# Strassen products for the last two chunks of four feed forward stages, and splits of 2048 columns

## The chip, the core and the metric

The kernel runs on one core of a Trainium2 chip. The metric is the device time of one execution in microseconds (us). The kernel before took 1417.25 us, the median of three runs (1417.22 to 1417.32).

## What is computed

Two transformer-like blocks one after the other on x (256 tokens x 1024), all in float32. The feed forward part is what the change is about:

```python
D_MODEL = 1024; SEQ = 256; D_FF = 2816
def swiglu(x, w_in, w_out):
    a, b = jnp.split(x @ w_in, 2, axis=-1)
    return (jax.nn.silu(a) * b) @ w_out
# first block, two layers l = 0, 1, each:
h = h + 0.5 * rms_norm(swiglu(rms_norm(h, g[0]), ffn1_w_in[l], ffn1_w_out[l]), g[1])
h = h + rms_norm(mixer_l(rms_norm(h, g[2])), g[3])
h = h + 0.5 * rms_norm(swiglu(rms_norm(h, g[4]), ffn2_w_in[l], ffn2_w_out[l]), g[5])
# second block: mod = silu(c) @ w_ada + b_ada, an attention/retention mixer, then
ffn = jnp.dot(jax.nn.silu(jnp.dot(h2, w_ffn_gate)) * jnp.dot(h2, w_ffn_up), w_ffn_down)
x = x + gate2 * ffn
```

## The kernel before

**Stages.** There are eight stages, 0 to 7. Stages 0, 2, 3, 5 and 7 are feed forward, 1 and 4 the mixers of the first block, 6 the mixer of the second. The tokens are two halves of 128 (tok 0 and 1), and these are the rows of every matmul's output.

**Units and half units.** All weights are streamed from HBM once, in units of 4 blocks of 128 rows x 512 columns (1 MB). `plan` lists the units in order. A unit goes to one of three ring buffers (`raw`, `load_unit`, L480), which SyncE (SP) loads when the unit three before it has been split. A unit has two half units (`subs`, index j, 1024 columns of SBUF). ScalarE writes `whi`, the float32r value of the half unit (`split_hi`, L508), and VectorE writes `wlo`, the rest (`split_lo`, L524). There are seven slots for half units (NSPL). Both engines run up to five half units (LOOK) ahead of the place in their own program where TensorE's half unit j stands (`ahead`). TensorE makes three matmuls of 512 columns for each block and token half: x high by w high, x high by w low, x low by w high (`products`, L700), so 12 for a half unit.

**A feed forward stage.** The inner 2 x 2816 columns are cut into 11 chunks of 256 + 256 columns (chunk c, two units, 4 half units). After a chunk ScalarE takes silu of one half (L1094) and VectorE multiplies by the other, the gate (L1100), which frees the chunk's PSUM bank. Every two chunks TensorE turns the result (`pe_hid_two`, L1155; the eleventh alone in `pe_hid`), ScalarE and VectorE split it into `gh` and `gl`. Then follows the down part, 22 half units, in groups; the last LAG half units make their tok 0 passes first, and the next stage's first transposes come between.

**Strassen in stage 7.** Two neighbouring chunks, 8 and 9, are one 256 x 1024 by 1024 x 1024 product, cut in 2 x 2 blocks and made from 7 products p1 to p7 instead of 8. `sequence` places one product after each of seven chunks. A product is one unit (12 matmuls in all, `pe_product`, L778). p2 goes through the ring. The others have a buffer of their own: `rows` (x1) for p1, p5, p6 and p4, `work` (x2) for p3 and p7. GpSimd (POOL) issues their loads (`pool_strassen`); for p5, p4 and p7 the DMA adds to what is in the buffer, in two halves. p6's weights are the sum of both buffers, which VectorE makes (`dve_t2`, L543). The sums of x are made in `dve_sx` and `dve_sx_lo` (2048 columns), and results are combined in `act_part` and `dve_combine`. Within such a stage all ordinary chunks use the same two PSUM banks, the products four others.

**The second block's modulation.** w_ada (24 MB) is loaded during stages 0, 2, 3 and 5 in 96 tiles, `adat`, through SP's queue, two buffers: a tile's issue waits until VectorE has added the tile two before it (`ada_add`, L618), which it does right after a split. Eight tiles are followed by a store, a reload and a chain of small sums (`ada_sum`, L621). `ada_units` says at which units; steps are 10 units apart.

Each engine's instructions are in program order, and a wait holds all behind it.

Of the kernel before, what the change touches and what calls it, by code (L numbers as in the profile page):

```python
# [115 lines left out]
def program(nc, T, const_at, out):  # L116
    ctx = ExitStack()
    with ctx:
# [25 lines left out]
        whi = [sb(f"whi{i}", 1024, F32R) for i in range(NSPL)]  # L144
        wlo = [sb(f"wlo{i}", 1024, F32R) for i in range(NSPL)]
# [136 lines left out]
        STRASSEN = (7,)  # L282
        PAIR = 8
# [221 lines left out]

        at = {"hi": 0, "lo": 0}
# [17 lines left out]
        def split_lo(e, upto):  # L524

            while at["lo"] < min(upto, NSUB):
                j = at["lo"]
                u, k, m, n = subs[j]
                if j in sum_before:
                    dve_t2(e, sum_before[j])  # L530
                e.wait_ge(*whi_made.at(j))
                e.tensor_tensor(split_of(wlo, j), raw_of(j), split_of(whi, j).bitcast(F32), ALU.subtract  # L532
                                ).then_inc(*wlo_made.up(j))
# [6 lines left out]

        sum_before = {JP[st, "p6"] - 3: st for st in STRASSEN}

# [311 lines left out]
        def pe_down(e, key, j0, XH, XL, nk, new, readers, at=None, late=None, lag=3, then=None):  # L854
# [18 lines left out]
            for i in range(len(order)):  # L873
# [6 lines left out]
                held.append(i)  # L880
                if i < len(order) - lag and not late or late and len(held) >= lag and i < len(order) - 1:
# [205 lines left out]
        def act_silu(e, st, c, tok):  # L1087
# [4 lines left out]
            if c >= 2 and tok == 0:  # L1092
                e.wait_ge(*hid_turned.at(st, turn_of(c - 2)))
# [19 lines left out]
        def act_silu_pair(e, st, tok):  # L1113
            e.wait_ge(*(product_done(st, "p4" if tok else "p2")))
            if tok == 0:
                e.wait_ge(*hid_turned.at(st, PAIR - 2))
# [11 lines left out]
        def turn_of(c):  # L1128

            return c if c == 10 else c - c % 2  # L1130

        def pe_hid(e, st):
            ps = tb.next(("hid", st, 10), (glo_made, st, 10))
            for done in tb.freed:
                e.wait_ge(*done)
            e.wait_ge(*gated.at(st, 10, 1))
# [4 lines left out]
            last.then_inc(*hid_turned.up(st, 10))  # L1141

        def pe_hid_two(e, st, c):
# [7 lines left out]
            for b in range(8):  # L1151
                n, j, tok = b // 4, b % 4 // 2, b % 2
                for half in range(2):
                    r = slice(half * 64, (half + 1) * 64)
                    last = e.transpose(pst[:, half * 512 + b * 64:half * 512 + (b + 1) * 64],  # L1155
                                       hid[(c + n) % 2][r, tok * 512 + j * P:tok * 512 + (j + 1) * P], ident[r, r])
# [8 lines left out]
        def act_ghi(e, st, c):  # L1165
            e.wait_ge(*hid_turned.at(st, c))
            if c == 10:
                e.activation(gh[:, 5120:5632], tb.of("hid", st, c)[:, :], ACT.Copy).then_inc(*ghi_made.up(st, c))
# [3 lines left out]
        def dve_glo(e, st, c):  # L1172
            e.wait_ge(*ghi_made.at(st, c))
            if c == 10:
                e.tensor_tensor(gl[:, 5120:5632], tb.of("hid", st, c)[:, :], gh[:, 5120:5632].bitcast(F32), ALU.subtract
# [6 lines left out]
        def pe_ffn_in(e, st):  # L1182
# [8 lines left out]
            for c in sequence(st)[2:]:  # L1191
                if c in BLOCK:
                    pe_product(e, st, c, base)
                    if c == "p4":
                        pe_hid_two(e, st, PAIR - 2)
                    continue

                def at(i, c=c):
                    if c % 2 == 0 and i == (3 if st in STRASSEN and c == 10 else 2):
# [11 lines left out]
        def pe_ffn(e, st):  # L1211
# [9 lines left out]
            pe_down(e, ("f", st), j1, gh, gl, 22,  # L1221
                    lambda q, tok: (ghi_made.at(st, turn_of(q // 2)), glo_made.at(st, turn_of(q // 2))), readers, at, lag=LAG[st],
# [1829 lines left out]
```

## Time and profile before

| | |
|---|---|
| median of 3 runs | 1417.25 us |
| the profiled execution | 1416.94 us |
| its span, first to last instruction | 1415.1 us |
| TensorE busy | 1401.8 us, 99% |
| VectorE busy | 956.5 us, 68% |
| ScalarE busy | 731.7 us, 52% |
| GpSimd busy | 160.1 us, 11% |
| moved by DMA | 288.24 MB, 204 GB/s |
| granted TensorE clock | 0.999 |

Busy times are unions of instructions of one engine. A matmul's own duration (390 ns at 512 columns) overlaps the next one's; the distance between starts is what it costs.

### The profile page before, as it was taken

To read this page: it belongs to the slowest core of one execution; us is meant where nothing else is said; L and a number is where in the kernel's file an instruction comes from. 1 tells how busy PE (TensorE), PEld (TensorE's weight loads), DVE (VectorE), ACT (ScalarE), POOL (GpSimd) and SP (SyncE) were. 2 spreads that over 40 slices of the span, in tenths; PEclk is the share of its full clock that TensorE was granted. 3 is DMA by queue.
4 is the path that set the end of the run, shared out by engine and by line. 5 is a ranking of instruction groups with operands and counts; after the bars stand their busy time and mean duration, and the time that the engine had idled before them with its cause. 6 is when DMAs were issued, how large, how long until landed. Compare 5 with 4: busy or idle time off the path is not lost.

```text
span 1415.1 us, 19090 instructions
## 1 busy us (share of the span) xinstructions
PE 1401.8 (99%) x7327; PEld 1147.2 (81%) x7327; DVE 956.5 (68%) x1307; ACT 731.7 (52%) x1050; POOL 160.1 (11%) x242
## 2 busy tenths in 40 slices
PE   9999999999999999999999999999999999999997
PEld 7888888688888888888878888888877788888886
DVE  6666567886676667665787757755568566786654
ACT  6444455564443445543665545445655634655542
POOL 1600010000000000000172100000542110011000
PEclk9999999999999999999999999999999999999999
DMA  9585755256876778868544688764845355588551
GB/s 318 199 253 198 262 203 207 68 171 207 251 242 215 231 228 265 252 210 264 187 150 148 203 210 256 255 211 140 238 160 197 121 178 179 171 242 211 178 209 59
DMA packets 234857, 288.24 MB, mean 204 GB/s; under 512 B 37076, under 2 KB 156672, under 8 KB 234768
## 3 DMA queue, kind: packets, MB, share of 16 engines
q1 hardware_dynamic: 232160, 281.48, 61.6%
q0 software_dynamic: 2208, 5.24, 1.8%
q8 instruction: 58, 0.95, 0.3%
q10 hardware_dynamic: 400, 0.31, 0.1%
q14 instruction: 31, 0.25, 0.1%
HBM read 282.80 MB, written 4.20 MB: 203 GB/s over the span
## 4 chain that ended last, share of the span: by engine, by line
PE 95%; DVE 2%; issue 1%; ACT 1%; POOL 0%; POOLq 0%; ACTq 0%; DVEq 0%
PE ps L706 29%; PE ps L709 28%; PE ps L707 28%; PE pst L974 1%; PE pst L1155 1%; DVE wlo L532 1%; PE pst L1468 1%; PE ps L813 0%; PE ps L812 0%; PE ps L811 0%; PE ps L1415 0%; ACT whi L521 0%; PE ps L679 0%; PE pst L1782 0%; PE pst L2355 0%
## 5 line engine op out<-in xcount | busy, mean ns | idle before, releaser
L532 DVE TENSOR_TENSOR wlo<-raw,whi 128x1024 fp32r<-128x1024 f32 (+2 forms) x468 | 558.2, 1224 | 257.7 <-ACT whi L521 255.9
L521 ACT ACTIVATE whi<-raw 128x1024 fp32r<-128x1024 f32 (+2 forms) x468 | 467.8, 1040 | 244.2 <-PE ps L709 97.4
L706 PE MATMUL ps<-whi,xh 128*128 128x512 f32 (+4 forms) x1406 | 551.5, 392 | 1.6 <-ACT xh L1013 0.6
L707 PE MATMUL ps<-wlo,xh 128*128 128x512 f32 (+4 forms) x1406 | 541.1, 385 | 0.0
L709 PE MATMUL ps<-whi,xl 128*128 128x512 f32 (+4 forms) x1406 | 532.7, 385 | 0.0
L706 PEld LDWEIGHTS ps<-whi,xh 128*128 128x128 f32 x1406 | 263.9, 188 | 60.6 <-issue 4.7
L709 PEld LDWEIGHTS ps<-whi,xl 128*128 128x128 f32 x1406 | 263.9, 188 | 53.6
L707 PEld LDWEIGHTS ps<-wlo,xh 128*128 128x128 f32 x1406 | 264.2, 188 | 49.8
L706 PE MATMUL ps<-whi,gh 128*128 128x512 f32 x440 | 172.0, 391 | 0.0
L707 PE MATMUL ps<-wlo,gh 128*128 128x512 f32 x440 | 171.2, 389 | 0.0
L709 PE MATMUL ps<-whi,gl 128*128 128x512 f32 x440 | 153.4, 389 | 0.0
L1094 ACT ACTIVATE hid<-ps,st 128x256 f32<-128x256 f32 x88 | 41.3, 473 | 151.0 <-PE ps L709 151.0
L914 POOL TENSOR_SCALAR st<-st 128x1 f32<-128x1 f32 x26 | 10.5, 405 | 903.1 <-ACT work L900 903.1
L1100 DVE SCALAR_TENSOR_TENSOR hid<-ps,st,hid 128x256 f32<-128x256 f32 x88 | 41.8, 482 | 87.8 <-ACT hid L1094 87.7
L709 PEld LDWEIGHTS ps<-whi,gl 128*128 128x128 f32 x440 | 82.6, 188 | 17.3
L706 PEld LDWEIGHTS ps<-whi,gh 128*128 128x128 f32 x440 | 82.6, 188 | 16.9
L707 PEld LDWEIGHTS ps<-wlo,gh 128*128 128x128 f32 x440 | 82.6, 188 | 16.8
L618 DVE SCALAR_TENSOR_TENSOR adaacc<-adat,scol,adaacc 128x512 f32<-128x512 f32 x84 | 62.7, 746 | 0.0
L1170 ACT ACTIVATE gh<-pst 128x1024 fp32r<-128x1024 f32 x25 | 25.5, 1020 | 20.9 <-PE pst L1155 20.7
L1179 DVE TENSOR_TENSOR gl<-pst,gh 128x1024 fp32r<-128x1024 f32 x25 | 30.5, 1221 | 8.1 <-ACT gh L1170 8.1
L900 ACT ACTIVATE work<-h 128x512 f32<-128x512 f32 x36 | 22.4, 627 | 20.3 <-DVE h L2249 18.9
L1613 DVE SCALAR_TENSOR_TENSOR Y<-cx,vcol,Y 128x256 f32<-128x256 f32 x79 | 32.4, 480 | 0.0
(306 smaller groups left out, 956.0 us busy)
## 6 DMA issues: line engine op xcount, KB each, us to landing
raw<-in_ffn_w_in_dram SPq DMA_DIRECT2D x174, 512.0 KB, 5.3
raw<-in_ffn_w_out_dram SPq DMA_DIRECT2D x40, 1024.0 KB, 5.5
raw<-in_w_in_dram SPq DMA_DIRECT2D x26, 1024.0 KB, 4.8
adat<-in_w_ada_dram SPq DMA_DIRECT2D x96, 256.0 KB, 2.8
raw<-in_hyb_w_in_dram SPq DMA_DIRECT2D x10, 1024.0 KB, 5.1
raw<-in_gla_w_in_dram SPq DMA_DIRECT2D x10, 1024.0 KB, 5.2
raw<-in_w_ffn_down_dram SPq DMA_DIRECT2D x10, 1024.0 KB, 5.0
raw<-in_w_ffn_gate_dram SPq DMA_DIRECT2D x18, 512.0 KB, 3.9
```

What stands on the lines that cost most here:

```text
L521: e.activation(split_of(whi, j), raw_of(j), ACT.Copy).then_inc(*whi_made.up(j))
L532: e.tensor_tensor(split_of(wlo, j), raw_of(j), split_of(whi, j).bitcast(F32), ALU.subtract).then_inc(*wlo_made.up(j))
L618: e.scalar_tensor_tensor(adaacc[:, :], adat[n % 2][:, :], sc, adaacc[:, :], ALU.mult, ALU.add).then_inc(*ada_added.up(c, k))
L706: e.matmul(ps[:, 0:n], a, whi_of(j, k), start=first and k == 0, stop=False)
L707: last = e.matmul(ps[:, 0:n], a, wlo_of(j, k), start=False, stop=False)
L709: last = e.matmul(ps[:, 0:n], b, whi_of(j, k), start=False, stop=final and k == subs[j][2] - 1)
L900: e.activation(spare[:, 0:src.shape[1]], src, ACT.Square, scale=scale, accum_out=col(2, "ss", key)[:, i:i + 1]).then_inc(*squares.up(key, i))
L1094: e.activation(hb[:, tok * 512 + 256:tok * 512 + 512], acc.of(st, JC[st, c], tok)[:, 0:256], ACT.Silu, scale=rstd(("h", st, tok)) if st < ...
L1100: e.scalar_tensor_tensor(hb[:, tok * 512:tok * 512 + 256], acc.of(st, JC[st, c], tok)[:, 256:512], rstd(("h", st, tok)) if st < 7 else 1.0 ...
L1170: e.activation(halves_of(gh[:, c * 512:(c + 2) * 512]), turned_halves, ACT.Copy).then_inc(*ghi_made.up(st, c))
L1179: e.tensor_tensor(halves_of(gl[:, x]), turned_halves, halves_of(gh[:, x]).bitcast(F32), ALU.subtract).then_inc(*glo_made.up(st, c))
L1613: e.scalar_tensor_tensor(y_of(b), cx_of(b, k), conv_w(b, k), y_of(b), ALU.mult, ALU.add).then_inc(*tap_made.up(b, k))
```

## The change

`STRASSEN` becomes (2, 3, 5, 7) and `PAIR` 9: chunks 9 and 10 are the pair in each of the four stages, p4 is the last thing before the down part, chunk 8 is turned alone and the pair's gates and transposes stand inside the down part. The products begin after chunk 2 instead of chunk 1. Rows for the norm gains of stages 2, 3 and 5 are then loaded behind the last product's split, as in stage 7 (`rows_free`). The positions of the `adat` tiles skip units with a buffer of their own. And in all five feed forward stages, from the third chunk to ten half units before the end, both halves of a unit are split by one operation of 2048 columns where their two slots are neighbours (`two`).

```diff
-        whi = [sb(f"whi{i}", 1024, F32R) for i in range(NSPL)]
-        wlo = [sb(f"wlo{i}", 1024, F32R) for i in range(NSPL)]
+        whix = sb("whi", NSPL * 1024, F32R)
+        wlox = sb("wlo", NSPL * 1024, F32R)
+        whi = [whix[:, i * 1024:(i + 1) * 1024] for i in range(NSPL)]
+        wlo = [wlox[:, i * 1024:(i + 1) * 1024] for i in range(NSPL)]
...
-        STRASSEN = (7,)
-        PAIR = 8
+        STRASSEN = (2, 3, 5, 7)
+        PAIR = 9
...
-                return (0, 1, "p1", 2, "p2", 3, "p5", 4, "p6", 5, "p3", 6, "p7", 7, "p4", 10)
+                return (0, 1, 2, "p1", 3, "p2", 4, "p5", 5, "p6", 6, "p3", 7, "p7", 8, "p4")
...
+        def two(j):
+            u, k, m, n = subs[j]
+            st = max(s for s in range(8) if J0[s] <= j)
+            return (st in (0, 2, 3, 5, 7) and J0[st] + 8 <= j < J0[st + 1] - 10 and k == 0 and n == 512
+                    and last_sub[u] == j + 1 and (j + 1) % NSPL)
...
-        ada_units = [u for st in (0, 2, 3, 5) for u in range(U0[st] + (8 if st == 0 else 0), U0[st + 1])]
+        ada_units = [u for st in (0, 2, 3, 5) for u in range(U0[st] + (8 if st == 0 else 0), U0[st + 1]) if u not in home]
...
         for c in range(12):
+            i = min(10 * c, c * (len(ada_units) - 13) // 11)
             for k in range(8):
-                ada_tiles[ada_units[10 * c + k]] = c, k
-            ada_sent[ada_units[10 * c + 11]] = c
-            ada_read[ada_units[10 * c + 12]] = c
-            ada_summed[ada_units[10 * c + 13]] = c
+                ada_tiles[ada_units[i + k]] = c, k
+            ada_sent[ada_units[i + 10]] = c
+            ada_read[ada_units[i + 11]] = c
+            ada_summed[ada_units[i + 12]] = c
...
+                if two(j) and j + 2 > upto:
+                    return
...
+                if two(j):
+                    if u in home and plan[u][0]:
+                        e.wait_ge(*(s_x1 if home[u] == "x1" else s_x2)[1].at(u))
+                    e.wait_ge(*mm[1].at(j + 1 - NSPL))
+                    whi_made.up(j)
+                    e.activation(pair_slots(whix, j), raw_unit(j), ACT.Copy).then_inc(whi_made.up(j + 1)[0], 2)
+                    at["hi"] += 2
+                    continue
...
+                if two(j):
+                    e.wait_ge(*whi_made.at(j + 1))
+                    wlo_made.up(j)
+                    e.tensor_tensor(pair_slots(wlox, j), raw_unit(j), pair_slots(whix, j).bitcast(F32), ALU.subtract
+                                    ).then_inc(wlo_made.up(j + 1)[0], 2)
...
-        sum_before = {JP[st, "p6"] - 3: st for st in STRASSEN}
+        sum_before = {JP[st, "p6"] - 4: st for st in STRASSEN}
...
             if st in STRASSEN:
-                acc.n += 4
+                acc.n += 2
...
-                if i == 2:
+                if i == (0 if st in STRASSEN else 2):
                     pe_hid(e, st)
+                if st in STRASSEN and i == 3:
+                    pe_hid_two(e, st, PAIR)
...
             pool_open(e, 2)
+            pool_strassen(e, 2)
             pool_open(e, 3)
+            pool_strassen(e, 3)
             pool_gla(e)
             pool_open(e, 5)
+            pool_strassen(e, 5)
```

In the down part of a Strassen stage the first two tok 1 passes are held behind the second tok 0 pass, and ScalarE's and VectorE's work on chunk 8 and on the pair moves in the same way as TensorE's.

## Rows read from the trace of the kernel before

**Rows 1.** The page: busy times by engine, and the chain that ended last.

```profile
PE 1401.8 (99%) x7327; PEld 1147.2 (81%) x7327; DVE 956.5 (68%) x1307; ACT 731.7 (52%) x1050; POOL 160.1 (11%) x242
...
PE ps L706 29%; PE ps L709 28%; PE ps L707 28%; PE pst L974 1%; PE pst L1155 1%; DVE wlo L532 1%; PE pst L1468 1%; PE ps L813 0%; PE ps L812 0%; PE ps L811 0%; PE ps L1415 0%; ACT whi L521 0%; PE ps L679 0%; PE pst L1782 0%; PE pst L2355 0%
```

**Rows 2.** Windows, stages 3 and 7: length, then PE, PEld, DVE, ACT, POOL busy; clock, DMA share, GB/s.

```profile
486.00:672.00 186.00, 186.00 (x893) 152.97 (x892) 126.53 (x157) 88.24 (x114) 4.19 (x8) 1.00 0.75 239
...
1220.00:1400.00 180.00, 180.00 (x864) 147.95 (x865) 116.09 (x129) 95.93 (x126) 11.15 (x11) 1.00 0.64 193
```

**Rows 3.** Timeline of ScalarE, down part of stage 7: start, us, instruction, idle before.

```profile
1364.48 1.06 ACT L521 ACTIVATE whi<-raw 128x1024 fp32r<-128x1024 f32 x1 [1.66 <-PE ps L709]
1367.20 1.06 ACT L521 ACTIVATE whi<-raw 128x1024 fp32r<-128x1024 f32 x1 [1.66 <-PE ps L709]
```

**Rows 4.** Lines asked one by one: 2048 columns on VectorE and ScalarE (min/median/max ns).

```profile
L605 DVE TENSOR_TENSOR sxl<-work,sxh x1: 2282/2282/2282, 1263.8 to 1263.8; 128x2048 fp32r<-128x2048 f32 x1
...
L601 ACT ACTIVATE sxh<-work x1: 1920/1920/1920, 1252.8 to 1252.8; 128x2048 fp32r<-128x2048 f32 x1
```

**Rows 5.** Timeline of VectorE, stage 7, from the end of chunk 2 to chunk 3's.

```profile
1263.77 2.28 DVE L605 TENSOR_TENSOR sxl<-work,sxh 128x2048 fp32r<-128x2048 f32 x1
...
1271.72 2.29 DVE L548 TENSOR_TENSOR rows<-rows,work 128x2048 f32<-128x2048 f32 x1
1273.93 1.22 DVE L532 TENSOR_TENSOR wlo<-raw,whi 128x1024 fp32r<-128x1024 f32 x1
1275.18 0.42 DVE L1100 SCALAR_TENSOR_TENSOR hid<-ps,hid 128x256 f32<-128x256 f32 x1
1276.54 0.43 DVE L1100 SCALAR_TENSOR_TENSOR hid<-ps,hid 128x256 f32<-128x256 f32 x1 [0.94 <-ACT hid L1094]
```

**Rows 6.** Timeline of VectorE, stage 2: an addition, then first and last of a chain of five.

```profile
341.38 0.75 DVE L618 SCALAR_TENSOR_TENSOR adaacc<-adat,scol,adaacc 128x512 f32<-128x512 f32 x1
342.04 0.42 DVE L625 TENSOR_TENSOR fold<-fold 128x256 f32<-128x256 f32 x1
...
343.49 0.16 DVE L634 TENSOR_TENSOR modc<-modc,vcol 128x4 f32<-128x4 f32 x1
```

**Rows 7.** POOL's issues, accumulating (L557, six) and plain (L559, four), and their landings.

```profile
L557 POOL DMA_DIRECT2D work<-in_w_ffn_up_dram x2: 1197/1446/1694, 1296.9 to 1297.6; - x2
...
DMA to landing us min/median/max: 5.7/8.3/11.5
...
L559 POOL DMA_DIRECT2D work<-in_w_ffn_up_dram x2: 754/755/756, 1266.4 to 1267.1; - x2
...
DMA to landing us min/median/max: 3.9/5.8/7.6
```

**Rows 8.** Timelines of POOL, ScalarE, VectorE: p7's issue, its split, chunk 6's gates.

```profile
1296.89 2.42 POOL L557 DMA_DIRECT2D work<-in_w_ffn_up_dram  x2 [11.98 <-DVE wlo L532]
...
1309.15 1.06 ACT L521 ACTIVATE whi<-work 128x1024 fp32r<-128x1024 f32 x1 [1.73 <-DMA work<-in_w_ffn_up_dram]
...
1317.73 0.42 DVE L1100 SCALAR_TENSOR_TENSOR hid<-ps,hid 128x256 f32<-128x256 f32 x1 [2.45 <-ACT hid L1094]
1319.09 0.42 DVE L1100 SCALAR_TENSOR_TENSOR hid<-ps,hid 128x256 f32<-128x256 f32 x1 [0.94 <-ACT hid L1094]
```

**Rows 9.** Windows: stage 7's products, and part of stage 3.

```profile
1290.50:1330.50 40.00, 40.00 (x191) 32.87 (x190) 25.37 (x26) 21.11 (x26) 2.42 (x2) 1.00 0.75 210
...
524.50:544.50 20.00, 20.00 (x90) 16.54 (x89) 14.47 (x17) 10.40 (x13) 0.00 (x0) 1.00 0.94 301
```

**Rows 10.** Timelines of ScalarE, VectorE and TensorE around chunk 2's second unit, stage 3.

```profile
517.74 2.01 ACT L521 ACTIVATE whi<-raw 128x1024 fp32r<-128x1024 f32 x2 [5.90 <-DMA raw<-in_ffn_w_in_dram]
...
518.83 2.36 DVE L532 TENSOR_TENSOR wlo<-raw,whi 128x1024 fp32r<-128x1024 f32 x2 [4.89 <-ACT whi L521]
...
523.60 0.50 PE L706 MATMUL ps<-whi,xh 128*128 128x512 f32 x1
```

More of the change, by code:

```diff
@@ L528, in split_lo @@
                 u, k, m, n = subs[j]
+                if two(j) and j + 2 > upto:
+                    return
                 if j in sum_before:
                     dve_t2(e, sum_before[j])
-                e.wait_ge(*whi_made.at(j))
-                e.tensor_tensor(split_of(wlo, j), raw_of(j), split_of(whi, j).bitcast(F32), ALU.subtract
-                                ).then_inc(*wlo_made.up(j))
+                if two(j):
[3 more added lines that the diff above has]
+                                    ).then_inc(wlo_made.up(j + 1)[0], 2)
+                    at["lo"] += 1
+                    j += 1
+                else:
+                    e.wait_ge(*whi_made.at(j))
+                    e.tensor_tensor(split_of(wlo, j), raw_of(j), split_of(whi, j).bitcast(F32), ALU.subtract
+                                    ).then_inc(*wlo_made.up(j))
                 at["lo"] += 1
@@ L880, in pe_down @@
                 held.append(i)
+                if key[1] in STRASSEN and i == 0:
+                    continue
+                if key[1] in STRASSEN and i == 1:
+                    one(held.pop(0), 1)
                 if i < len(order) - lag and not late or late and len(held) >= lag and i < len(order) - 1:
@@ L1115, in act_silu_pair @@
             if tok == 0:
-                e.wait_ge(*hid_turned.at(st, PAIR - 2))
+                e.wait_ge(*hid_turned.at(st, PAIR - 1))
             e.activation(pair_of(hidx, tok, 256), both(acc.of(st, "ba"[tok])), ACT.Silu,
@@ L1126, in dve_gate_pair, with turn_of, alone @@
                                    ).then_inc(*gated.up(st, PAIR, tok))
-        def turn_of(c):
+        def turn_of(st, c):
+            if st in STRASSEN:
+                return PAIR - 1 if c == PAIR - 1 else PAIR if c >= PAIR else c - c % 2
             return c if c == 10 else c - c % 2
+        def alone(st):
+            return PAIR - 1 if st in STRASSEN else 10
         def pe_hid(e, st):
-            ps = tb.next(("hid", st, 10), (glo_made, st, 10))
+            c = alone(st)
+            ps = tb.next(("hid", st, c), (glo_made, st, c))
             for done in tb.freed:
                 e.wait_ge(*done)
-            e.wait_ge(*gated.at(st, 10, 1))
+            e.wait_ge(*gated.at(st, c, 1))
             for j in range(2):
@@ L1140, in pe_hid @@
                                        hid[0][:, tok * 512 + j * P:tok * 512 + (j + 1) * P], ident)
-            last.then_inc(*hid_turned.up(st, 10))
+            last.then_inc(*hid_turned.up(st, c))
         def pe_hid_two(e, st, c):
@@ L1245, in act_ffn @@
                         act_part(e, st, COMBINE[c])
-                    if st in STRASSEN and (c, i) == (2, 1):
+                    if st in STRASSEN and (c, i) == (3, 1):
                         act_sx(e, st)
@@ L1253, in act_ffn @@
                 act_begin(e, JD[st] + i)
-                if i == 2:
-                    act_ghi(e, st, 10)
+                if i == (0 if st in STRASSEN else 2):
+                    act_ghi(e, st, alone(st))
+                if st in STRASSEN and i == 0:
+                    act_silu_pair(e, st, 0)
+                    act_silu_pair(e, st, 1)
+                if st in STRASSEN and i == 3:
+                    act_ghi(e, st, PAIR)
         def dve_ffn(e, st):
@@ L1273, in dve_ffn @@
                     dve_begin(e, JC[st, c] + i)
-                    if st in STRASSEN and i == 3 and c in (5, 7):
+                    if st in STRASSEN and i == 3 and c in (6, 8):
                         dve_combine(e, st, COMBINE[c])
@@ L1279, in dve_ffn @@
                 dve_gate(e, st, c, 1)
-                if st in STRASSEN and c == 1:
+                if st in STRASSEN and c == 2:
                     dve_sx(e, st)
-                if st in STRASSEN and c == 2:
+                if st in STRASSEN and c == 3:
                     dve_sx_lo(e, st)
@@ L1285, in dve_ffn @@
                 dve_begin(e, JD[st] + i)
-                if i == 2:
-                    dve_glo(e, st, 10)
+                if i == (0 if st in STRASSEN else 2):
+                    dve_glo(e, st, alone(st))
+                if st in STRASSEN and i == 0:
+                    dve_gate_pair(e, st, 0)
+                    dve_gate_pair(e, st, 1)
+                if st in STRASSEN and i == 3:
+                    dve_glo(e, st, PAIR)
         hyb_gate = sig("hyb_gate")
```

34 lines of the change are left out of this document (15 added, 19 removed).

## The prediction

> **What bounds the kernel now.** I read the page first: TensorE is busy for 99% of the span, VectorE 68%, ScalarE 52%, and 95% of the chain that ended last is TensorE's own work, nearly all of it in the three matmul lines of `products` [rows 1]. The stretches come next: TensorE has no idle time in stage 3 (two more stages, 2 and 5, read alike) or in stage 7, while VectorE is busy for 68 and 64% and the DMA engines for 75 and 64% [rows 2]. So a matmul taken out is time taken out, as long as whatever feeds it stays ahead. How far ahead is what the remaining views are for: near the end ScalarE's split waits each time for TensorE to free a slot, 2.72 us after the last one [rows 3]. That is the price of one half unit (12 matmuls of 512 columns), 0.2267 us a matmul.
>
> Terms: a half unit is one 1024-column split; hi is ScalarE's split, lo is VectorE's; c3.1 is the second unit of chunk 3; a product is one of p1 to p7.
>
> **Term 1, matmuls removed.** Two chunks cost 2 x 8 half-unit passes of 6 matmuls, 96 in all; seven products of 12 cost 84. Stage 7 has them already, stages 2, 3 and 5 get them: 3 x 12 = 36 matmuls, 36 x 0.2267 = 8.16 us off an engine with no slack [rows 3]. Transposes per stage stay the same in number (five double ones and one single). Taken: -8.16.
>
> **Term 2, splits and sums added.** Products need 14 half units where two chunks needed 8: 18 splits more. With them come per stage the sums of x (5 operations), the 2048-column `sxl` (2.28 us) and the 2048-column sum of weights (2.29 us), two combines and 2 MB more to load [rows 4, 5]. All of this is beside TensorE's work, so it costs only where it makes something late. Average load first, for one stage from p1 to p4: TensorE 6 chunks x 10.88 + 7 x 2.72 + 3 transposes x 0.9 = 87 us. VectorE: 38 splits x 1.14 = 43; 13 `adaacc` additions of 0.7 = 9; a chain of `fold` sums 2; sums of x 3.9; `sxl` and weights 4.6; `gl`, gates, combines about 11; 73 us, or 84%. It fits on average, but not with much room at its worst place, and there the products have a rule of their own: all chunks of a stage use the same two PSUM banks, so the gates of a chunk must be done before the next chunk starts, one product (2.72 us) later. Whatever delays VectorE by more than that stops TensorE. I looked at the two places where VectorE can wait.
>
> **Place A: the sum of weights (`dve_t2`) after chunk 4's splits.** In stage 7 VectorE goes from `sxl` (1263.77) without a pause through splits, the sum at 1271.72 and another split to the gate of the chunk, which starts at 1275.18, 1.36 us before the last gate [rows 5]. In the new order this segment has `sxl` 2.2, c4.1, p5 and c5.0 at 2.27 each, the sum 2.2 and `gl` 1.14, 12.4 us, plus one or two additions of 0.68 (stage 5 also a `fold` chain, 1.6 [rows 6]): 13.1 to 15.4 us, of 13.6 (chunk and product) + 0.9 (transposes) = 14.5 us from one chunk's end to the next. It starts 1.0 to 1.3 us after the chunk's end, so the first gate ends 0.1 to 2.7 us past the next end; allowed are 2.72. The sum also waits for p3's DMA, which POOL issues when `sxl` is done. Plain loads from POOL landed in 3.9 to 7.6 us, and this one did not hold VectorE up [rows 7, 5]; the sum is wanted about 5 us after its issue. Bounds per stage: 0 (landing at 5) and 2.5 us (landing at 7.6). I take 0.13 for each of three stages, near the lower end, as the row of the same transfer shows no wait: +0.4.
>
> **Place B: p7, added onto its buffer by DMA.** Accumulating transfers from POOL landed in 5.7 to 11.5 us [rows 7]. For p7 POOL began at 1296.89, and the second half of the split started only at 1309.15, after 1.73 us of waiting for that landing: 12.3 us [rows 8]. Now the split is one operation, so nothing of it starts before 1309.15: hi 1.92, lo 2.28, then c7.0 2.28 and `gl` 1.14 gives 1316.9, and the gate that began at 1317.73 [rows 8] is not touched in stage 7. In stages 2, 3 and 5 there are two additions more (1.4), so 1318.3 and the first gate done at 1318.8. The chunk ends at about 1318.6 (its last gate starts 0.45 later, at 1319.09 [rows 8]), and with the product's 2.72 the gate has until 1321.3: 2.5 us of room. Beyond that each us costs one. The DMA share was 0.75 around there in stage 7, and 0.94 in a stretch of stage 3 with `adat` loads [rows 9]. Landing slower by 0 gives 0; by the ratio of the shares, 12.3 x 0.94 / 0.75 = 15.4, 3.1 more, it gives 0.6 per stage. I take 0.2 per stage: +0.6.
>
> The Trainium skill ("DMA: Bandwidth & Descriptors", Anatomy of one DMA) gives about 2.0 us + bytes / 436 GB/s for a DMA from GpSimd. For 512 KB that would be 3.2 us, an estimate from the page; places A and B would then never wait and both terms would be 0. The trace disagrees, with 5.7 to 11.5 us for the accumulating ones.
>
> **Term 3, stage openings.** p1's load (1 MB) now lands in the opening of stages 2, 3 and 5, while the row broadcast (0.5 MB) leaves it and goes behind p4's split. The tightest place of all stages is c2.1 in stage 3: its hi waits 5.90 us for a DMA and starts at 517.74, lo of its first half ends 1.22 us after 518.83, at 520.05, of the second at 521.19, and TensorE takes it at 523.60: 3.5 us of room [rows 10]. The merged unit ends 1.92 + 0.1 + 2.28 = 4.3 us after the start, 522.0, and 0.5 MB more at 301 GB/s [rows 9] are 1.7 us: 523.7, a tenth late. In stages 2 and 5 the same unit had more room. Bounds 0 and 2.5 us (the whole MB, unshared, in all three less their room); I take +0.3.
>
> **Term 4, merged splits.** By the condition in `two`, 113 units get one hi and one lo of 2048 columns (21 in stage 0, 23 in each other). Two lo of 1024 take 2.36 us from start to end, one of 2048 2.28 to 2.29 [rows 4, 10]: 0.07 x 113 = 8 us less of VectorE, hidden by TensorE. Against it the first half is ready 1.1 us later and the unit 0.85 later (4.3 instead of 3.45, [rows 10]). Elsewhere a unit is split several us ahead (in the down part five half units, 13.7 us [rows 3]), so 0. Bounds: 0.85 at the opening of five stages, 4.3 us, and -0.5 (VectorE reaches a gate sooner). The Trainium skill ("VectorE: DVE Perf Modes", on the fixed extra latency per instruction) says that SBUF operations pay a fixed cost each, so fewer, larger ones are better; by that rule VectorE has more room and places A and B shrink. The trace agrees in sign, with 0.07 us a pair.
>
> **Term 5, the rest: 0.** The end of a Strassen stage: after p4 TensorE turns chunk 8, then does six passes of 1.36 us before it needs the pair's gates; silus and gates of 512 columns (0.68 each) are done in under 4. Its row load holds SyncE until p4's split, some 8 us before chunk 8 ends, and the second down unit then has 15 us to arrive. `adat` steps are 9 or 10 units apart instead of 10, the last chain comes at the end of stage 5, ten us before the stage boundary. Stage 7 only changes its order. Together within 0.5 us of nothing either way.
>
> **Sum.** -8.16 + 0.4 + 0.6 + 0.3 = -6.9 us. The profiled execution took 1416.94 us, 1.8 more than its span; it lies 0.3 under the median of the runs. 1416.94 - 6.9 = 1410.0, and 1410.4 against the median of 1417.25.
>
> **Rivals.**
> - All hidden: places A and B and the openings cost nothing. For it: stage 7 ran the products with no gap on TensorE. Against it: no `adat` traffic and no additions there. 1417.25 - 8.2 = 1409.1.
> - The split's latency: 0.85 us at the openings of five stages and the upper bound at the openings, 4.3 + 2.5, on top of 8.16 less: 1415.8, no measurable change. For it: rows 10. Against it: only one place in the trace is that tight.
> - Late release of banks, the slower side: p7 (and p4, p5 in the same way) lands so late that the gates miss the product's cover in each of three stages. It decides from a landing of 12.3 + 2.5 + 2.7 = 17.5 us, where the gain is spent; at 19 us it is 4.2 + 2.5 (place A at its bound) per stage, 20 - 8.2 = 12 us slower, 1429. For it: DMA at 0.94 in rows 9, and that the two halves must now both have landed. Against it: this one was the slowest of POOL's ten [rows 7].
> - The change does not do what it says: TensorE spends the saved time in small waits at the banks, since each chunk of the three stages is now bound to two of them; 18 chunks x 0.4 us cancel the gain: 1416.5.
>
> **Numbers.** This kernel's measurement can tell about 0.2% (2.8 us) from no change: faster is below 1414.4, slower above 1420.1. Forecast (1409.2 to 1413.5) 0.53, all hidden 0.25, split's latency 0.09, banks 0.05, late release 0.08. Faster: 0.53 + 0.25 + 0.02 of the latency case = 0.80; same 0.12; slower 0.08. The range reaches from the first rival less the half us of term 5 to the second: 1408.5 to 1416.0.
>
> **What would show it.** Right: TensorE's lines 36 matmuls fewer, VectorE's busy time up by less than 20 us, stages 2, 3 and 5 each about 2 us shorter (186 to 184). Term A: VectorE idle before the sum of weights, with POOL's or the DMA's name. Term B: ScalarE's split of `work` waiting for a DMA for more than 2 us in stages 2, 3 and 5, and TensorE waiting for `hid` gates. Term 3: a wait of TensorE for `wlo` some 35 us into a stage. It is wrong if TensorE's idle time rises by over 5 us, or if it stays where it was.

## The result: 0.9% slower, and the profile after

The changed kernel takes 1429.22 us, the median of four runs (1427.65 to 1430.87), against 1417.24 for the kernel before (1416.02 to 1417.32): a ratio of 1.0087, 95% interval 1.0069 to 1.0104. The forecast was 1410.4 and faster; the range ended at 1416.0. The profiled execution took 1430.87 us, 13.9 more than that of before.

The page of the changed kernel: busy times, and the chain that ended last.

```profile
PE 1401.3 (98%) x7291; PEld 1143.9 (80%) x7291; DVE 991.6 (69%) x1233; ACT 745.1 (52%) x961; POOL 191.7 (13%) x272
...
PE 75%; DVE 8%; DMA 7%; issue 4%; ACT 4%; SPq 1%; POOL 0%; POOLq 0%; ACTq 0%; DVEq 0%
```

TensorE has 36 matmuls fewer (7291 instead of 7327), as forecast, and yet is busy for as long as before [rows 1]. And its share of the chain has fallen from 95% to 75%: VectorE and the DMAs now stand between its stretches. Its idle time in the span rose from 13.3 to 27.7 us, by 14.4, where the forecast called itself wrong above 5. The windows of stages 3 and 7 (length; PE, PEld, DVE, ACT, POOL busy; clock, DMA share, GB/s) say where:

```profile
486.00:672.00 186.00, 180.78 (x853) 147.39 (x852) 131.55 (x135) 89.22 (x94) 14.56 (x18) 0.98 0.78 233
1232.00:1412.00 180.00, 179.77 (x863) 147.47 (x862) 115.26 (x106) 95.33 (x105) 11.95 (x13) 1.00 0.63 194
```

Stage 7 is as full as it was. Stage 3 was full [rows 2] and now has 5.2 us without TensorE work and a granted clock of 0.98. What TensorE waited for, in the whole kernel (us in total, times, longest):

```profile
PE ps L744 <- DVE hid L1142: 9.1, 4, 3.4
PE ps L744 <- ACT xh L1055: 2.6, 4, 1.5
PE ps L744 <- DVE wlo L564: 2.6, 1, 2.6
...
PE ps L744 <- DVE wlo L570: 0.6, 1, 0.6
...
PE ps L849 <- DVE wlo L564: 0.5, 1, 0.5
```

Before, no wait of TensorE was longer than 1.1 us and none was for the gates (`hid`, now L1142). `xh` was 0.6 there and `wlo` 0.5, so the new waits are 9.1 + 2.0 + 3.2 = 14.3 us. The clock is the other loss. Windows of TensorE behind or around its three longest waits (length, PE busy; clock, DMA share, GB/s):

```profile
362.36:366.30 3.94, 3.94 (x10) 0.57 1.05 349
...
564.00:575.00 11.00, 7.74 (x22) 0.69 0.35 109
864.00:868.00 4.00, 4.00 (x11) 0.57 0.75 237
```

A granted clock of 0.57 over 3.94 us means that most of it ran at 0.5, the lower level (1.2 GHz). Length times what is missing of 1.00 gives 1.7 + 3.4 + 1.7 = 6.8 us; 0.3 of it lies inside the wait of stage 3. Two small waits have grown by 0.8 together (L1402 and L1203). So 14.3 + 0.8 + 6.5 - 8.2 = 13.4 of the 13.9 us.

**How one of these waits comes about.** The chain of waits of the changed kernel in stage 2, between the end of chunk 3 and the start of chunk 4 (start, us, what; lines left out are marked):

```profile
347.48 2.28 DVE wlo L564
349.76 0.67 DVE adaacc L656
350.45 0.34 SPq L681
350.84 0.43 SPq L504
...
356.93 1.93 ACT whi L544
...
361.16 0.75 DVE adaacc L656
361.91 0.41 DVE hid L1142
362.36 0.55 PE ps L744
362.90 0.43 PE ps L745
```

And two rows of its timelines there, VectorE's and TensorE's:

```profile
358.95 2.29 DVE L564 TENSOR_TENSOR wlo<-raw,whi 128x2048 fp32r<-128x2048 f32 x1 [4.73 <-ACT whi L544]
...
362.36 0.55 PE L744 MATMUL ps<-whi,xh 128*128 128x512 f32 x1 [3.42 <-DVE hid L1142]
```

Read it upwards from TensorE. It waited for the gates; they stood in VectorE's program behind an `adat` addition (361.16) and a split (358.95), for which VectorE had idled 4.73 us; that split waited for ScalarE's, which began at 356.93; SP issued the load's two halves at 350.84 and 351.3, and they landed 4.6 and 5.5 us after that, the second at 356.8. The issue came straight behind an `adat` tile (L681, 350.45). The tile's issue waits for VectorE's addition, which ended at 350.43. So VectorE's own order decides when SP may load the unit that VectorE waits for next, and the gates stand behind that unit. TensorE had finished the product and could not start chunk 4, because both of the stage's PSUM banks wait for the gates. After 3.42 us of this its matmuls are 0.43 us apart instead of 0.23.

In stage 3 it is the sum of weights (`dve_t2`, here L586). Timelines of POOL and VectorE:

```profile
552.88 1.50 POOL L597 DMA_DIRECT2D work<-in_ffn_w_in_dram  x2 [23.65 <-DVE sxl L643]
...
561.99 2.29 DVE L586 TENSOR_TENSOR rows<-rows,work 128x2048 f32<-128x2048 f32 x1 [4.55 <-DMA work<-in_ffn_w_in_dram]
564.20 2.29 DVE L564 TENSOR_TENSOR wlo<-raw,whi 128x2048 fp32r<-128x2048 f32 x1
566.40 1.22 DVE L1227 TENSOR_TENSOR gl<-pst,gh 128x1024 fp32r<-128x1024 f32 x1
567.54 0.87 DVE L1142 SCALAR_TENSOR_TENSOR hid<-ps,st,hid 128x256 f32<-128x256 f32 x2
```

p3's load took 9.1 us from its issue to the sum (the forecast's worst was 7.6, [rows 7]); VectorE idled 4.55 us and then had a split, `gl` and the gates to do. TensorE waited 3.26 us, until 568.07, and stood at the lower level for 6.8 us, from 567.5 to 574.3. In the other two stages the sum cost TensorE little in this execution: VectorE idled 1.70 us for p3 in stage 2 and TensorE waited for nothing behind it; in stage 5 VectorE did not idle before it at all and TensorE waited 1.00 us.

### The profile page after: what moved, and what is told of

Read it like the earlier page. It is cut to its first block, busy times and chain, and to the rows that moved or that the text cites. A ratio compares the mean times of both kernels' runs of the same rounds, so it can differ in the third digit from the quotient of the medians.

```text
span 1429.0 us, 18919 instructions
## 1 busy us (share of the span) xinstructions
PE 1401.3 (98%) x7291; PEld 1143.9 (80%) x7291; DVE 991.6 (69%) x1233; ACT 745.1 (52%) x961; POOL 191.7 (13%) x272
## 4 chain that ended last, share of the span: by engine, by line
PE 75%; DVE 8%; DMA 7%; issue 4%; ACT 4%; SPq 1%; POOL 0%; POOLq 0%; ACTq 0%; DVEq 0%
PE ps L744 22%; PE ps L747 21%; PE ps L745 21%; DMA raw<-in_ffn_w_in_dram 3%; DVE wlo L570 3%; DMA raw<-in_ffn_w_out_dram 2%; PE ps L851 1%; PE ps L849 1%; PE ps L850 1%; ACT whi L544 1%; PE pst L1203 1%; ACT whi L549 1%; PE pst L1016 1%; DVE wlo L564 1%; DMA raw<-in_gla_w_in_dram 1%
## 5 line engine op out<-in xcount | busy, mean ns | idle before, releaser
L744 PE MATMUL ps<-whi,xh 128*128 128x512 f32 (+2 forms) x1310 | 516.8, 395 | 15.3 <-DVE hid L1142 9.1
L745 PE MATMUL ps<-wlo,xh 128*128 128x512 f32 (+2 forms) x1310 | 506.3, 386 | 0.0
L747 PE MATMUL ps<-whi,xl 128*128 128x512 f32 (+2 forms) x1310 | 497.8, 387 | 0.0
L570 DVE TENSOR_TENSOR wlo<-raw,whi 128x1024 fp32r<-128x1024 f32 (+4 forms) x264 | 316.4, 1225 | 172.6 <-ACT whi L549 171.0
L549 ACT ACTIVATE whi<-raw 128x1024 fp32r<-128x1024 f32 (+4 forms) x264 | 262.6, 1030 | 152.5 <-DMA raw<-in_ffn_w_out_dram 65.4
L747 PEld LDWEIGHTS ps<-whi,xl 128*128 128x128 f32 x1310 | 247.4, 189 | 50.5
L564 DVE TENSOR_TENSOR wlo<-raw,whi 128x2048 fp32r<-128x2048 f32 x93 | 213.1, 2293 | 104.3 <-ACT whi L544 104.3
L745 PEld LDWEIGHTS ps<-wlo,xh 128*128 128x128 f32 x1310 | 247.7, 189 | 46.6
L544 ACT ACTIVATE whi<-raw 128x2048 fp32r<-128x2048 f32 x93 | 177.8, 1914 | 121.5 <-DMA raw<-in_ffn_w_in_dram 51.3
L1142 DVE SCALAR_TENSOR_TENSOR hid<-ps,st,hid 128x256 f32<-128x256 f32 x76 | 35.3, 480 | 45.0 <-ACT hid L1136 44.8
L1218 ACT ACTIVATE gh<-pst 128x1024 fp32r<-128x1024 f32 x25 | 25.5, 1020 | 24.2 <-PE pst L1203 24.2
L564 DVE TENSOR_TENSOR wlo<-rows,whi 128x2048 fp32r<-128x2048 f32 x14 | 32.0, 2286 | 1.8 <-ACT whi L544 1.8
```

What stands on the lines that cost most here:

```text
L544: e.activation(pair_slots(whix, j), raw_unit(j), ACT.Copy).then_inc(whi_made.up(j + 1)[0], 2)
L549: e.activation(split_of(whi, j), raw_of(j), ACT.Copy).then_inc(*whi_made.up(j))
L564: e.tensor_tensor(pair_slots(wlox, j), raw_unit(j), pair_slots(whix, j).bitcast(F32), ALU.subtract).then_inc(wlo_made.up(j + 1)[0], 2)
L744: e.matmul(ps[:, 0:n], a, whi_of(j, k), start=first and k == 0, stop=False)
L745: last = e.matmul(ps[:, 0:n], a, wlo_of(j, k), start=False, stop=False)
L747: last = e.matmul(ps[:, 0:n], b, whi_of(j, k), start=False, stop=final and k == subs[j][2] - 1)
```

## The experiments

Theory Q: the gates and splits come late because of the order of work in SP's and VectorE's queues around the products. Rival M: the cost is in the merged splits. Each ratio is against the kernel before on the same chip; its medians beside the runs were 1416.96 to 1417.24 us, so a difference between medians of two experiments carries some 0.3 us of that, besides the spread of each. The edits are to the changed kernel unless it says otherwise.

**One half of the change each: e1, merged splits alone, and e2, products alone.** e1 is the kernel before with `two`, the merged operations, and the sum of weights of stage 7 one half unit later, e2 the changed kernel with

```diff
-            return (st in (0, 2, 3, 5, 7) and ...
+            return (st in () and ...
```

> The kernel before with the merged splits alone (units of two half units split by one operation of 2048 columns; the sum of weights in stage 7 stands before c4.1 instead of inside c4.0). Theory Q (a split whose weights come late stands in VectorE's queue in front of a chunk's gates, and with only two PSUM banks for the chunks TensorE must wait for these): no new products, so no such wait, 1417 us within 1.5. Rival M (the merged split is at fault, since it starts when both halves have landed and ends 0.85 us later): slower by 4 us or more, 1421 and up.

> The changed kernel with single splits again. Theory Q: the waits stay, a little shorter for the 0.85 us of a unit; 1423 to 1429 us. Rival M: the loss goes and the removed matmuls show, 1410 to 1414 us.

Measured: e1 1422.70 us (ratio 1.0045, 1.003 to 1.0059), e2 1426.40 (1.0064, 1.0049 to 1.0079). Both halves are slower than before by themselves. For e2, Q had it right: without merging the 36 fewer matmuls still lose 9 us. For e1, M had it right. Most of e1's loss is at one place in stage 5. SP's queue and ScalarE's split there:

```profile
838.39 0.43 SPq L3027 DMA_DIRECT2D gate_rows<-modc  x1
838.87 1.26 SPq L503 DMA_DIRECT2D raw<-in_ffn_w_in_dram  x2
...
854.64 1.91 ACT L543 ACTIVATE whi<-raw 128x2048 fp32r<-128x2048 f32 x1 [12.76 <-DMA raw<-in_ffn_w_in_dram]
```

The unit issued just behind the store of `gate_rows` (its elements are of 4 bytes) is split 15.8 us after its issue. In the kernel before the same store stands in front of the same unit, which was split 12.6 us after its issue (835.87 to 848.43), and TensorE had some 4.9 us of room there; with the merged split, which also waits for the whole unit, TensorE waited 2.8 and 1.6 us. Two suspects follow: the store, and the merged split's own latency.

**SP's order: e3.** The `adat` tile is issued behind the next ring unit's load instead of in front of it.

```diff
+            held = [0]
...
-                load_ada(e, u)
+                if u not in home:
+                    load_ada(e, held[0])
+                    held[0] = u
```

> The changed kernel, with SyncE issuing each adat tile after the next ring unit's load instead of before it, so that no weight load waits for an addition of VectorE. Theory Q with the adat wait as the cause of the late loads: the waits of 3.4 us in stage 2 (c4.0) and 2.6 and 1.0 us in stage 5 (c4.1) go, and with them two stretches of 3.4 us at half clock (another 3.4 us): about 1419 us. Rival L (what is late is the landing of GpSimd's transfers): no change, 1428 to 1430 us.

Measured: 1421.21 us (1.0025, 1.0016 to 1.0034), 8.0 us better than the changed kernel. The stage 2 stall of the chain above is gone. What is left above 1 us, besides two at the start that the kernel before has too, is a wait of 1.1 us in stage 3, 1.5 at the opening of stage 5, and 1.2 and 3.64 in stage 5, the last with the clock at 0.5 after it.

**VectorE's order: e4, e11, e13, e6.** e4 puts the sum of weights behind the gates of chunk 4, with nothing else changed:

```diff
-        sum_before = {JP[st, "p6"] - 4: st for st in STRASSEN}
+        sum_before = {JP[st, "p6"] - 2: st for st in STRASSEN}
```

> The changed kernel, with the sum of weights (dve_t2) moved behind chunk 4's gates, before c5.1's split. In the trace it waited 4.6 us for p3's landing in stage 3, and the gates behind it cost TensorE 3.3 us and 6.8 us at half clock. Theories Q and L: these 3.3 + 3.4 us go, 1422 to 1423 us; the waits of stages 2 and 5 stay. Rival M: no change.

Measured: 1426.72 us (1.0062, 1.0047 to 1.0077), only 2.5 better, a miss. The stall of stage 3 went, but the profiled run had 3.10 us of waiting in stage 2 and 3.76 in stage 5, for a split's `wlo`, with 6.8 us at clock 0.5 around its end: SP's order was still the old one. Between the profiled executions the edit took away 3.26 us of waiting and 3.1 of lower clock in stage 3; stage 5 took 1.4 back (a wait 1.2 us longer, 1.2 more by the lower clock, the wait of 1.00 gone), and stage 3 got a new wait of 1.2 in front of a product (L849). With e3's order underneath, the same edit does something else. e11 is e3's order with `dve_sx` moved behind chunk 3's first split (theories S: the sums of x in front of the splits cost; W: the sum of weights in front of the gates costs, as it waits for p3):

```diff
-                if st in STRASSEN and c == 2:
-                    dve_sx(e, st)
...
+                    if c == "p1":
+                        dve_sx(e, st)
```

> Experiment 3's kernel with the sums of x behind c3.1's split alone (the sum of weights stays in front of c5.0). Experiment 6, with both, was 6.3 us faster than experiment 3, where 1.5 were expected. Theory S (the sums of x, 4 us in front of a split, start the delay that runs on through the loads): nearly all of the 6.3, 1415 to 1416 us. Rival W (the sum of weights waiting for p3's landing in front of gates): little, 1420 to 1421 us, and the wait of over 3 us in stage 5 is there.

> Experiment 3's kernel with two orders of VectorE changed as well: the sums of x behind c3.1's split, the sum of weights behind chunk 4's gates. Gate store where it was. Theory Q: in experiment 3 stages 2 and 3 have only 0.5 and 1.1 us of such waits left, so 1 to 1.5 us less, 1420 us; stage 5's 6.5 us stay, if theory G is right. If the 3.6 us of stage 5 come from the order of VectorE instead, 1414 us.

> Two of the three orders on the changed kernel: the adat tile issued behind the ring unit's load, and the sum of weights behind the gates; the sums of x stay behind chunk 2. With all three orders the time was 1414.9, with the first alone 1421.2, with the first and the later sums of x 1423.9. If the sum of weights is the whole of the third order's gain and the sums of x are indifferent (theory W): 1414 to 1416.5. If the sums of x behind chunk 3's split are needed as well, since they still push the gates of chunk 3 back (theory S): 1418 to 1421, with a wait of TensorE for hid near 360 or 850.

| | order of SP | sum of weights late | sums of x late | us | ratio, interval |
|---|---|---|---|---|---|
| e3 | yes | no | no | 1421.21 | 1.0025 (1.0016 to 1.0034) |
| e11 | yes | no | yes | 1423.89 | 1.0054 (1.0036 to 1.0072) |
| e13 | yes | yes | no | 1414.58 | 0.9984 (0.9975 to 0.9993) |
| e6 | yes | yes | yes | 1414.88 | 0.9989 (0.998 to 0.9998) |

The sum of weights is worth 6.6 us once SP's order is right (e3 to e13). The sums of x are worth nothing (e13 to e6) and cost 2.7 where the sum of weights still stands in front (e3 to e11; e11 is above what either theory gave it): p3's load is then issued later, at 547.66 instead of 544.57 in stage 3. S falls. Of W the first half stands: the sum costs where it stands in front of the gates. I had put e6 at 1420 and was 5 us off.

The wait for p3 is only a part of it. The longest wait of e3, in stage 5, VectorE's rows and TensorE's:

```profile
847.11 2.29 DVE L564 TENSOR_TENSOR wlo<-raw,whi 128x2048 fp32r<-128x2048 f32 x1 [4.48 <-ACT whi L544]
...
855.44 2.29 DVE L586 TENSOR_TENSOR rows<-rows,work 128x2048 f32<-128x2048 f32 x1
...
861.04 0.87 DVE L1142 SCALAR_TENSOR_TENSOR hid<-ps,st,hid 128x256 f32<-128x256 f32 x2
```

```profile
861.57 0.50 PE L744 MATMUL ps<-whi,xh 128*128 128x512 f32 x1 [3.64 <-DVE hid L1142]
```

p3 was issued at 842.94, 12.5 us before the sum, and the sum waited for nothing. What was late was a ring unit's load (4.48 us of idle), and the sum's 2.29 us, a `fold` chain and the splits stood between it and the gates. So of e3's 5.2 us of waiting for gates 3.6 are of this kind and 1.07, in stage 3, are behind an idle of 4.08 us for p3. The wait of 3.64 us is absent from the profiled executions of e13 and e6, which move the sum, and of e5 below, which moves a store: either edit removes it, so their gains overlap.

Where the sum stands behind the gates, VectorE's rows of e6 in stage 3:

```profile
555.69 0.48 DVE L1142 SCALAR_TENSOR_TENSOR hid<-ps,st,hid 128x256 f32<-128x256 f32 x1 [0.53 <-ACT hid L1136]
557.05 0.49 DVE L1142 SCALAR_TENSOR_TENSOR hid<-ps,st,hid 128x256 f32<-128x256 f32 x1 [0.88 <-ACT hid L1136]
557.45 2.28 DVE L586 TENSOR_TENSOR rows<-rows,work 128x2048 f32<-128x2048 f32 x1
```

The gates now wait for ScalarE alone, and the sum for nothing: p3 has landed by then.

**The store and the fold chain: e5, e7, e12.** e5 is e3 with the first `gate_rows` store moved into stage 6. e7 is e6 with that and with one `ada_sum` two units later, out of the opening of stage 5. e12 is e1 with the store in stage 4.

The store of e5 and e7:

```diff
-                    if u in (U0[5] + 10, U0[6] + 8):
+                    if u in (U0[6] + 4, U0[6] + 8):
...
```

The store of e12:

```diff
-                    if u in (U0[5] + 10, U0[6] + 8):
+                    if u in (U0[4] + 10, U0[6] + 8):
```

The fold chain of e7:

```diff
-            ada_summed[ada_units[i + 12]] = c
+            ada_summed[ada_units[i + 12 + 2 * (c == 8)]] = c
```

> Experiment 3's kernel (adat tiles issued behind the next load) with the first store of gate_rows (1024 elements of 4 bytes, SyncE's queue) moved out of stage 5 into the start of stage 6. Theory G: in stage 5 this store sits in front of c4's or c5's load and makes it land late, which is what the two waits of TensorE there (1.2 and 3.6 us) and the 3.4 us at half clock (1.7 us) come from: 1421.2 - 6.5 = 1414.7 us. Rival: the loads of stage 5 are late because of the accumulating transfers or of the adat traffic, and the store is harmless: 1420 to 1422 us.

> All of it: adat tiles behind the next load, both orders of VectorE, the gate store in stage 6, and the chain of fold sums that falls on stage 5's first unit two units later (it cost 1.5 us at the opening). Merged splits stay. Theories Q and G: no TensorE wait of over 1 us is left in the feed forward stages, and the 36 matmuls show: 1409.5 to 1411.5 us.

> Experiment 1's kernel (the kernel before with merged splits alone) with the first gate store in stage 4. Experiment 1 lost 5.5 us, of which 4.4 are two TensorE waits in stage 5, on the load issued right behind this store. Theory G and M together (a merged split eats the room, the store takes the rest): these 4.4 go, 1418 us. Rival M alone: 1421 us or more.

Measured: e5 1417.02 us (1.000, 0.9991 to 1.0009), e7 1413.01 (0.9969, 0.9958 to 0.9981), e12 1419.04 (1.0017, 1.0008 to 1.0026). Moving the store gave 4.2 us in e5 (against e3; 6.5 were expected) and 3.7 in e12 (against e1). The rows of e12 answer to those of e1:

```profile
838.64 0.98 SPq L503 DMA_DIRECT2D raw<-in_ffn_w_in_dram  x2
...
845.68 1.92 ACT L543 ACTIVATE whi<-raw 128x2048 fp32r<-128x2048 f32 x1 [3.46 <-DMA raw<-in_ffn_w_in_dram]
```

7.0 us from issue to split instead of 15.8, with the store gone from in front of it; the two halves landed 4.8 and 6.5 us after their issues instead of 13.4 and 14.9. But e12 is still 2.1 us slower than before, and e7 missed its 1409.5 to 1411.5.

**Single against merged with all else right: e8, and where: e14.** e8 is e7 with single splits. e9 is e8 with the store in stage 4 instead of 6. e14 is e9 with merged splits in stages 2, 3 and 5 only (69 of the 113 units).

> As experiment 7, with single splits. If a merged split only hurts where loads are late (theory Q), no difference from experiment 7 now, within 1 us: 1409.5 to 1411.5 us. If it hurts by itself (rival M), 3 us or more faster than experiment 7.

> Experiment 8's kernel (single splits, all orders changed) with the first gate store in stage 4 instead of stage 6, where it put a wait of 1.3 us in front of L2516 (experiments 5, 7 and 8 all have one there of 0.9 to 1.4). Theory G: a load behind this store lands late wherever it is, and in stage 4 the DMA engines have room; the 1.3 us go: 1409.1 us, which is 1417.25 less 36 matmuls. Rival: the wait in stage 6 has another cause: 1410.4 us.

> The best version (1409.6, single splits everywhere) with the merged splits in stages 2, 3 and 5 alone, 69 of the 113. If merged splits cost through the loop of load, split, addition and next load, which only stages with adat tiles have to the full (theory L): 1411.5 to 1413, all of the 2.6 us that lay between single and merged. If the cost is spread over all merged units evenly: 1411.2. If it lies in stages 0 and 7: 1409.6 to 1410.2.

Measured: e8 1410.43 us (1409.54 to 1411.05; ratio 0.9951, 0.9936 to 0.9966), 2.6 below e7, and no run of the one lies among the other's. e9 1409.65 us (1409.52 to 1410.89; 0.9952, 0.9939 to 0.9964). e14 1411.67 (1410.75 to 1412.35; 0.9962, 0.9949 to 0.9974), 2.0 above e9. The 0.8 us from e8 to e9 lie within the spread of the two. So merging costs 2 to 2.6 us although it takes work from VectorE, and most of that in the three stages; whether it is spread evenly over the units (1411.2 expected) or sits in those stages (1411.5 up) these intervals do not tell. Where it costs is shown in part: the profiled execution of e7 has a wait of 0.75 us for gates in stage 2 and one of 1.43 for ScalarE's `hid` (L1159) in stage 5 that e8's has not; e9, with single splits, has 0.85 of the second. The pages of e7, e8 and e9:

```profile
PE 1394.9 (99%) x7291; PEld 1140.0 (81%) x7291; DVE 993.7 (70%) x1233; ACT 747.5 (53%) x961; POOL 190.4 (13%) x272
```

```profile
PE 1393.5 (99%) x7291; PEld 1139.6 (81%) x7291; DVE 1002.2 (71%) x1346; ACT 755.9 (54%) x1074; POOL 195.1 (14%) x272
```

```profile
PE 1393.5 (99%) x7291; PEld 1139.8 (81%) x7291; DVE 1000.8 (71%) x1346; ACT 756.2 (54%) x1074; POOL 193.5 (14%) x272
...
PE 94%; DVE 2%; issue 2%; DMA 1%; ACT 1%; SPq 0%; POOL 0%; POOLq 0%; ACTq 0%
```

TensorE is busy 8.3 us less than before [rows 1], as Term 1 says, and the chain is 94% TensorE again. e9 is the best version: 0.48% faster than the kernel before, 1.4% faster than the change as it was made. It has the 36 fewer matmuls, single splits and five moves in the order (SP's tiles, the sum of weights, the sums of x, the store, one fold chain). Its stage 3, in the window of [rows 2], is full again:

```profile
486.00:672.00 186.00, 186.00 (x893) 152.93 (x892) 142.53 (x168) 98.78 (x125) 16.38 (x18) 1.00 0.79 238
```

VectorE is busier there than in the changed kernel (142.5 us against 131.6) and holds nobody up.

**e10: e9 without SP's order.**

> Experiment 9's kernel with the adat tiles in front of the next load again, as in the changed kernel: this one cause put back into a kernel without the others. Theory Q: the loads wait for additions of VectorE, c4 of stages 2 and 3 come late again; 2 to 5 us slower than experiment 9. If the order of VectorE, the store and the merged splits were all there was to it: no difference within 0.5 us.

Measured: 1412.79 us (0.9968, 0.9957 to 0.998), 3.1 slower than e9. The same edit was worth 8.0 in the changed kernel: the causes overlap. In which wait the 3.1 us lie is not shown: the profiled execution is the fastest of the six (1411.45), has no wait for gates above 0.6 us, and one of 1.53 for ScalarE's `hid` (L1159) in stage 3.

## Why the prediction was wrong, step by step

One path through the medians, from the changed kernel to the best: 1429.2, less 8.0 (SP's order, e3), less 6.6 (sum of weights, e13), plus 0.3 (sums of x, e6), less 1.9 (store and fold chain, e7), less 2.6 (single splits, e8), less 0.8 (store in stage 4, e9), is 1409.6. Another order would share them out otherwise, as e4, e5 and e10 show, and the last 0.8 and the 0.3 are no more than the spread.

**Term 1 (-8.16) was right.** 36 matmuls fewer, and 1401.8 - 1393.5 = 8.3 us less TensorE time where nothing disturbs it.

**Term 2, place A (+0.4) is the step that failed first, by its size and in part by its mechanism.** The mechanism that was named: the sum of weights waits for p3, in front of the gates, on two banks. Its bounds were 0 and 2.5 us a stage, and I took 0.13, "near the lower end, as the row of the same transfer shows no wait". That row was of stage 7, which has no `adat` traffic. Measured: moving the sum behind the gates gave 6.6 us (e3 to e13), and in stage 3 of the changed kernel VectorE's wait was 4.55 us, TensorE's 3.26 and the lower clock took 3.1 more. But it is not 2.2 in each of three stages, and not all for p3: the stall of 3.64 us in e3's stage 5 had p3 long landed. There another line of the term failed. It added up VectorE's work between two chunks' ends as if no split in it waited for its load, and even so came to a first gate up to 2.7 us past the end, of 2.72 allowed, in stage 5, the one with a `fold` chain. With VectorE idle for 4.48 us for a ring unit's load, that room was gone. The landing bound of 7.6 us was too low as well: the two halves of p3 landed 7.2 and 8.2 us after their own issues in stage 3, 9.1 after the first. And the price did not count what TensorE's clock does behind such a wait.

The Trainium skill ("DMA: Bandwidth & Descriptors", Anatomy of one DMA) gives about 2.0 us + bytes / 436 GB/s for a DMA from GpSimd, so an estimate of 3.2 us for each 512 KB half of p3. The trace disagrees for plain loads too, with those 7.2 and 8.2 us.

**Place B (+0.6) did not happen.** ScalarE's split of p7 waited for its landing for more than 2 us, as the forecast's sign said; in stage 3, from the timelines of POOL and ScalarE:

```profile
590.15 2.42 POOL L595 DMA_DIRECT2D work<-in_ffn_w_in_dram  x2 [12.37 <-DVE wlo L570]
...
602.58 1.92 ACT L544 ACTIVATE whi<-work 128x2048 fp32r<-128x2048 f32 x1 [3.56 <-DMA work<-in_ffn_w_in_dram]
```

12.4 us from issue to split here, 11.6 and 14.6 in stages 2 and 5, all under the 15.4 of the forecast's upper bound; TensorE waited for nothing there.

**What no term had: SP's queue.** This is the larger omission. The forecast followed POOL's and VectorE's order, and of `adat` it said only that the steps were 9 or 10 units apart (Term 5, 0). It did not follow the loop that the chain of stage 2 shows: addition on VectorE, tile on SP, load behind it, landing, split, gates. In the kernel before the loop was there and no gate made TensorE wait; that it has no room now because of the sums of x, `sxl` and the added splits in front of the additions is read from the chain of stage 2, and no run takes them out alone. e3 puts it at 8.0 us in the changed kernel, e10 at 3.1 where all else is mended. Term 5 took the pair's silus and the moved additions at 0: for one silu (L1159) TensorE waited 0.7 to 1.6 us in the traces of ten experiments. With a fold chain at the opening of stage 5 it waited 1.5 us for `xh`, and in e7, where the chain stands elsewhere, it did not. The store of `gate_rows` was in no term. It stands where it stood before the change, and costs 3.7 to 4.2 us once the room behind it is used up (e5, e12); in the kernel before TensorE waited for nothing there.

**Term 3 (+0.3) came out at its lower bound, 0.** TensorE did not wait some 35 us into a stage. In e1, the merged unit made it wait 0.8 us at that place in stage 3 (a tenth of a us was forecast there).

**Term 4 (0) was 2 to 2.6 us.** The 0.85 us by which a merged unit is ready later was said to be hidden by the distance at which units are split ahead. That distance is an average too. In the loop above, a later split is a later addition, a later tile and a later next load; that this is how the 2 to 2.6 us come about is argued, not shown. The Trainium skill ("VectorE: DVE Perf Modes", on the fixed extra latency per instruction) is right about the work: VectorE is 8.5 us less busy in e7 than in e8. The time went the other way, +2.6 us.

**The clock (no term).** 6.5 us of the loss, from the three windows above.

**The load of VectorE.** I wrote that its busy time would rise by less than 20 us. It rose by 35.1. The working itself had 18 splits x 1.14 = 20.5, and 3 x (3.9 + 4.6) = 25.5, less 8: 38. The sign was set without adding up the terms that stood above it, and 38 us on three stages would have made the room look smaller.

**The rivals.** "Late release of banks" gave 1429, the number that was measured, by luck, and the right end of the chain (gates too late for the product's cover). Its place and its price were wrong: it is not p7, which landed in time, but p3 and the ring's loads behind `adat` tiles, and 6.5 of its us are the clock. "The split's latency" had a cost of the right sign (2 to 2.6 us where it allowed 4.3). "All hidden" (1409.1) is what e9 reaches once the order is mended; "does not do what it says" fell, since in e8 and e9 TensorE has no small waits at the banks. With 0.08 and 0.09 the first two had far too little: several additions use the same 2.72 us of room, and I judged each by itself.

**Open.** Why the wait of stage 5 grew in e4 when only the sum of weights had moved; how a merged split comes to cost time; what the rule of two banks for the chunks costs by itself, which was not tried; and what the store costs in stage 6 or 4 (a wait of 1.3 us at L2516 in e8, which e9 has not; e9's of 1.3 at L1832 was 1.0 in the kernel before).

## What to carry to other kernels

Where an operation is added to a stage with little room, follow the whole loop in which it stands (the load's issue, what is in front of it in that queue, what frees that, the split, the next issue), and add up all additions against one room instead of testing each alone. An operation that waits for a DMA goes behind whatever releases TensorE, not in front of it. Fewer, larger operations saved 8.5 us of busy time here on an engine that had spare time anyway, and the kernel became 2 to 2.6 us slower.

## What the runs showed of the hardware

**Waits of TensorE of 2 to 4 us mostly cost more than themselves.** In the changed kernel the waits of 3.42 and 2.55 us were each followed by 3.4 us at a granted clock of 0.5, around the end of that of 3.26 it was 6.8 us; in e11 one of 2.45 us by 3.4, in e13 one of 2.06 by 3.4. All traces together have 12 waits between 2.06 and 3.80 us, and 11 have such a stretch behind or around their end. The other one, of 2.80 us in e1, has none. The window behind e11's wait, and the one behind e1's:

```profile
562.07:565.30 3.23, 3.23 (x8) 2.58 (x9) 3.23 (x4) 0.00 (x0) 0.00 (x0) 0.50 0.92 310
```

```profile
859.00:862.40 3.40, 3.40 (x15) 2.81 (x16) 3.40 (x5) 1.65 (x2) 0.00 (x0) 1.00 0.51 143
```

8 matmuls in 3.2 us against 15 in 3.4. Waits of 1.6 us and less were in no run followed by the lower level.

**A small store delays the load behind it.** With the store of `gate_rows` in front (1024 elements of 4 bytes), the halves of a 1 MB unit landed 13.4 and 14.9 us after their issues and the unit was split after 15.8; without it they landed after 4.8 and 6.5 and the split came after 7.0 (e1 and e12, the same place). In the kernel before, with the store, the halves took 10.7 and 11.9 us.
